# Gates spread by transfers, columns made by transposes, row fills issued later, and a reordered last slot in a two-layer encoder kernel

## The reference

```python
mod = c_act @ ada_w[layer] + ada_b[layer]
sh_m, sc_m, g_m, sh_f, sc_f, g_f = split(mod, 6)
h = rms_norm(x, norm_mix_g[layer]) * (1 + sc_m) + sh_m
x = x + g_m * token_mixer(h, ...)      # 2304-column projection, window + differential attention, w_out
h = rms_norm(x, norm_ffn_g[layer]) * (1 + sc_f) + sh_f
y = swiglu(h, ...) if layer == 0 else moe_swiglu(h, ...)   # dense 3584 wide; or top 2 of 8 experts
x = x + g_f * y
# at the end: rms_norm(x, final_g)
```

## Time and profile before

| | |
|---|---|
| median of three runs | 1755.93 us |
| the profiled execution, its own time | 1757.38 us |
| its span, first to last instruction | 1755.6 us |
| mean granted TensorE clock | 0.963 |
| PE / DVE / ACT / POOL busy | 1639.4 / 1302.5 / 1024.1 / 29.7 us (93 / 74 / 58 / 2%) |
| DMA | 544.83 MB, 310 GB/s over the span |

### The profile page before, as it was taken

One profiled execution on the slowest core, in us unless ns is written; L12 is line 12 of the kernel. 1 busy time (PEld: TensorE's weight loads), 2 busy tenths in 40 slices (PEclk: granted clock), 3 DMA queues, 4 the chain that ended last, 5 costly groups with the idle time before them and its releaser, 6 DMA issues.

```text
span 1755.6 us, 20351 instructions
## 1 busy us (share of the span) xinstructions
PE 1639.4 (93%) x7699; PEld 1314.7 (75%) x7700; DVE 1302.5 (74%) x997; ACT 1024.1 (58%) x760; POOL 29.7 (2%) x35
## 2 busy tenths in 40 slices
PE   3988889999798778999999999999999999999996
PEld 1755678878684667888888888888888888888884
DVE  2856644355475568898888888988898888888885
ACT  2324443354334435777777777767777767677772
POOL 0000000000000001000000000000000000000002
PEclk7899799999899689999999999999999999999998
DMA  9578576436168228999999999999999999999992
GB/s 366 199 290 331 214 291 227 152 143 223 64 216 334 98 97 349 368 381 389 372 391 378 370 386 373 387 388 374 387 378 376 394 362 387 385 376 390 380 373 73
DMA packets 161471, 544.83 MB, mean 310 GB/s; under 512 B 9704, under 2 KB 12432, under 8 KB 155280
## 3 DMA queue, kind: packets, MB, share of 16 engines
q1 hardware_dynamic: 154416, 528.01, 78.7%
q10 hardware_dynamic: 5856, 11.99, 1.9%
q0 software_dynamic: 1152, 4.19, 0.7%
HBM read 528.43 MB, written 15.73 MB: 310 GB/s over the span
## 4 chain that ended last, share of the span: by engine, by line
PE 84%; DVE 7%; ACT 3%; DMA 2%; issue 2%; POOL 1%; ACTq 1%; DVEq 0%; POOLq 0%
PE ps L1562 25%; PE ps L1564 25%; PE ps L1563 25%; DVE weights_lo L953 2%; PE ps L1521 2%; PE ps L1809 2%; DMA lamv<-in_lam_k_dram 1%; PE ps L1641 1%; DVE tmp L1051 1%; DMA weights<-in_ada_w_dram 1%; PE ps L1629 1%; PE ps L1533 1%; PE ps L1552 0%; PE ps L1617 0%; PE ps L1780 0%
## 5 line engine op out<-in xcount | busy, mean ns | idle before, releaser
L1249 DVE TENSOR_TENSOR raw_lo<-raw,raw_hi 128x4096 fp32r<-128x4096 f32 x188 | 831.2, 4425 | 143.2 <-ACT raw_hi L783 140.7
L783 ACT ACTIVATE raw_hi<-raw 128x4096 fp32r<-128x4096 f32 x188 | 683.3, 3635 | 221.4 <-PE ps L1564 221.4
L1562 PE MATMUL ps<-raw_hi,hT_hi 128*128 128x512 f32 x1008 | 397.5, 394 | 0.8 <-DVE hT_lo L1439 0.8
L1564 PE MATMUL ps<-raw_hi,hT_lo 128*128 128x512 f32 x1008 | 393.6, 390 | 0.0
L1563 PE MATMUL ps<-raw_lo,hT_hi 128*128 128x512 f32 x1008 | 393.1, 390 | 0.0
L1564 PEld LDWEIGHTS ps<-raw_hi,hT_lo 128*128 128x128 f32 x1008 | 189.7, 188 | 40.0
L1562 PEld LDWEIGHTS ps<-raw_hi,hT_hi 128*128 128x128 f32 x1008 | 189.9, 188 | 38.9 <-DVE hT_lo L1439 1.0
L1563 PEld LDWEIGHTS ps<-raw_lo,hT_hi 128*128 128x128 f32 x1008 | 190.0, 189 | 38.1
L1562 PE MATMUL ps<-raw_hi,m_actT_hi 128*128 128x512 f32 x504 | 196.2, 389 | 1.2 <-DVE m_actT_lo L1255 1.2
L1564 PE MATMUL ps<-raw_hi,m_actT_lo 128*128 128x512 f32 x504 | 196.3, 390 | 0.0
L1563 PE MATMUL ps<-raw_lo,m_actT_hi 128*128 128x512 f32 x504 | 196.1, 389 | 0.0
(11 more groups left out here) (223 smaller groups left out, 1352.5 us busy)
## 6 DMA issues: line engine op xcount, KB each, us to landing
raw<-in_moe_w_gate_dram SPq DMA_DIRECT2D x126, 1024.0 KB, 6.0
raw<-in_moe_w_up_dram SPq DMA_DIRECT2D x126, 1024.0 KB, 8.3
raw<-in_moe_w_down_dram SPq DMA_DIRECT2D x126, 1024.0 KB, 7.0
weights<-in_ada_w_dram SPq DMA_DIRECT2D x24, 2048.0 KB, 10.7
weights<-in_w_in_dram SPq DMA_DIRECT2D x8, 2048.0 KB, 9.9
weights<-in_ffn_w_gate_dram SPq DMA_DIRECT2D x14, 1024.0 KB, 6.4
weights<-in_ffn_w_up_dram SPq DMA_DIRECT2D x14, 1024.0 KB, 8.6
weights<-in_ffn_w_down_dram SPq DMA_DIRECT2D x7, 2048.0 KB, 10.3
```

Source lines behind the costliest of these rows:

```text
L783: act.activation(raw_hi[HIGH_OF[p]][:], raw[RAW_OF[p]][:], ACT.Copy).then_inc(m_hi, 1)
L1249: dve.tensor_tensor(raw_lo[r][:], raw[r][:], raw_hi[h][:].bitcast(F32), ALU.subtract).then_inc(m_lo, 1)
L1562: pe.matmul(dst, stat_hi, hi, start=start, stop=False, skip_group_check=True)
L1564: return pe.matmul(dst, stat_lo, hi, start=False, stop=stop, skip_group_check=True)
```

## The change

It has six parts. Gates: POOL issues eight transfers for each gate (`spread_gate`), each from one group of 32 partitions of modrow to 32 partitions of `gate`; the matmuls, the four ACT copies and PE's wait are gone, and DVE waits for the transfers (`gate_mix`, `gate_ff`). Columns: PE transposes whole pieces of modrow into a PSUM bank of its own for each round, and DVE copies one of 32 columns. ACT: `straight("out", layer, 1)` stands right after `split_transposed`. Fills: ACT issues the two fills after its part of the first dense block, not before it. Slots: SP issues the gate and up loads of phase 1 ahead of the load of the rows. End: `gated_output` comes ahead of `earlier_slots`.

```diff
+        COLUMN_ROUNDS = [((0, 0, 0),), ((0, 1, 0), (0, 2, 1), (1, 0, 6)), ((1, 1, 0), (1, 2, 1))]
...
@@ sync: slot
                 for n in range(NPH):
+                    for p in GU_AT[n]:
+                        room(p)
+                        load_gate_up(e, n, p)
                     if n == 1:
                         sp.wait_ge(rows_put, 16 * 2 * NT)
...
-                    for p in GU_AT[n]:
-                        room(p)
-                        load_gate_up(e, n, p)
@@ gpsimd
+            def spread_gate(layer, which):
+                r, done = 1 + which, (gate_mix, gate_ff)[which]
+                pool.wait_ge(mod_ready, 3 * layer + r + 1)
+                for h in range(2):
+                    g = 2 * which + h
+                    for j in range(4):
+                        pool.dma_start(gate[32 * j:32 * j + 32, which, 512 * h:512 * h + 512],
+                                       modrow[32 * g:32 * g + 32, r, :]).then_inc(done, 16)
             for layer in range(DEPTH):
                 norm(2 * layer)
                 for t in range(NT):
+                    spread_gate(layer, t)
                     pool.wait_ge(dms_done, NT * layer + t + 1)
@@ scalar
-            def gates(layer):
-                for i in range(4):
-                    act.wait_ge(gates_ps, 4 * layer + i + 1)
-                    act.activation(gate[:, i // 2, (i % 2) * 512:(i % 2) * 512 + 512], ps[:, 4 + i, :],
-                                   ACT.Copy).then_inc(gates_ready, 1)
...
                 one(0, False)
+                act.dma_start(x_rows.rearrange("s p n -> p s n"),
+                              fing[:].unsqueeze(1).broadcast_to([P, N_SLOT + 1, D])).then_inc(rows_filled, 16)
+                act.dma_start(y_rows[N_EXP - 1:].rearrange("s p n -> p s n"),
+                              fing[:].unsqueeze(1).broadcast_to([P, MAX_OVER + 1, D])).then_inc(rows_filled, 16)
...
                 split_transposed(3 * layer + 1)
-                gates(layer)
+                straight("out", layer, 1)
...
                     act.wait_ge(cols_ps, 2)
+                    act.wait_ge(gate_mix, 8 * 16)
+                    act.wait_ge(gate_ff, 8 * 16)
...
-                straight("out", layer, 1)
...
                 if not layer:
-                    act.dma_start(x_rows ...)
-                    act.dma_start(y_rows ...)
                     dense()
@@ vector
-                for layer, (a, b) in NEW_KINDS[n]:
-                    i = dve.tensor_copy(modc[:, layer, a:b], ps[:, 0, KD * a:KD * b].rearrange(
-                        "p (a k) -> p a k", a=b - a))
+                for layer, r, bank in COLUMN_ROUNDS[n]:
+                    i = dve.tensor_copy(modc[:, layer, 2 * r:2 * r + 2, :].rearrange("p a (b i) -> p (a b) i", i=4),
+                                        ps[:, bank, :].rearrange("p (i g x) -> p g i x", g=4, x=32)[:, :, :, 0])
...
                 act_turned(slots * NPH, WIDE[3])
+                gated_output(slots + (-1), slots * CHUNKS)
                 earlier_slots()
-                gated_output(slots + (-1), slots * CHUNKS)
...
-                dve.wait_ge(gates_ready, 4 * layer + 4)
+                dve.wait_ge(gate_mix, 8 * 16 * (layer + 1))
                 mixed(layer)
@@ tensor
+                for _, r, bank in COLUMN_ROUNDS[n]:
                     for i in range(4):
-                        mm = pe.matmul(ps[:, 0, 16 * r + i:16 * r + i + 13:4], modrow[:, r, i * P:i * P + P],
-                                       ident[:, 0:P:32], start=True, stop=True)
+                        mm = pe.transpose(ps[:, bank, i * P:i * P + P], modrow[:, r, i * P:i * P + P], ident[:])
...
                 mod_columns(layer + 1)
-                gates(layer)
-                pe.wait_ge(gates_ready, 4 * layer + 4)
                 for c in range(OUT_CHUNKS):
+                    if c:
+                        pe.wait_ge(cols_ready, layer + 2)
                     project("out", layer, c, 3 * layer + 1)
```

More of the change, by code:

```diff
@@ L332, in build @@
         ada_used, mod_ready, cols_ps, cols_ready = sem("ada_used"), sem("mod_ready"), sem("cols_ps"), sem("cols_ready")
-        gates_ps, gates_ready = sem("gates_ps"), sem("gates_ready")
+        gate_mix, gate_ff = sem("gate_mix"), sem("gate_ff")
         sq_done, ms_done, rstd_done, xn_done = sem("sq_done"), sem("ms_done"), sem("rstd_done"), sem("xn_done")
@@ L916, in _ @@
                 if not layer:
-                    act.dma_start(x_rows.rearrange("s p n -> p s n"),
-                                  fing[:].unsqueeze(1).broadcast_to([P, N_SLOT + 1, D])).then_inc(rows_filled, 16)
-                    act.dma_start(y_rows[N_EXP - 1:].rearrange("s p n -> p s n"),
-                                  fing[:].unsqueeze(1).broadcast_to([P, MAX_OVER + 1, D])).then_inc(rows_filled, 16)
                     dense()
@@ L1334, in dense_out @@
             def dense_out():
+                dve.wait_ge(gate_ff, 8 * 16)
                 for t in range(NT):
@@ L1488, in _ @@
             dve.memset(done_mark[:], 0.0).then_inc(y_stored, 16)
+            dve.wait_ge(gate_ff, 8 * 16 * DEPTH)
             first_input(0)
@@ L1526, in mod_columns @@
             def mod_columns(n):
-                rounds = ((0,), (1, 2, 0), (1, 2))[n]
                 pe.wait_ge(mod_ready, (1, 4, 6)[n])
-                for r in rounds:
+                for _, r, bank in COLUMN_ROUNDS[n]:
                     for i in range(4):
-                        mm = pe.matmul(ps[:, 0, 16 * r + i:16 * r + i + 13:4], modrow[:, r, i * P:i * P + P],
-                                       ident[:, 0:P:32], start=True, stop=True)
+                        mm = pe.transpose(ps[:, bank, i * P:i * P + P], modrow[:, r, i * P:i * P + P], ident[:])
                 mm.then_inc(cols_ps, 1)
-            def gates(layer):
-                for i, chunk in enumerate((4, 5, 10, 11)):
-                    g, r = chunk % 4, chunk // 4
-                    pe.matmul(ps[:, 4 + i, :], ones[32 * g:32 * g + 1, :], modrow[32 * g:32 * g + 1, r, :],
-                              start=True, stop=True).then_inc(gates_ps, 1)
             def transpose_all(n):
```

## The result

The changed kernel takes 1729.08 us, the median of four runs (1727.17 to 1731.18), against 1755.51 for the kernel before on the same chip: ratio 0.9852, 95% interval 0.9838 to 0.9866.

The account below looks back on a forecast made before the run. PE was taken to bound the kernel (busy 93% of the span, 84% of the wait chain). Terms -6.1 - 5.6 - 0.9 - 3.2 - 1.6 + 2.0 - 4.3 = -19.7 took 1757.38 to 1737.7, less 1.45: 1736 us, range 1730 to 1743.

Parts of the forecast that it names:

- Columns and gates: Between PE's last x transpose and the output projection: the gap shrinks to the new transposes, gaining 6.1 and 5.6 us.
- The clock at the output projections: Start of the output projection in both layers: the sum left the clock as it was, counting no gain.
- the rival that named this effect: Output projections: the clock rises by the first matmul, saving 5.3 us over both layers, for 1730.7 us; chance 0.10.
- First columns: First modulation columns: four transposes take 0.98 us where four matmuls took 1.87, gaining 0.9 us.
- Fills leave block 0: First dense block: PE's wait falls from 4.24 to 1.0 us, gaining 3.2, and the clock dip goes, gaining 1.6.
- Fills come to block 2: Dense block 2: the fills share the rate with weight loads and the second load comes late, costing 2.0 us.
- Gate transfers: POOL in attention: sixteen issues a layer at 0.98 + 0.30 to 1.95 us each do not delay rstd_d; cost nothing.
- slot loads: Expert slots: weights loaded ahead of the rows give nothing, since the load was already there in time.
- POOL's case: Rival in attention: issues take longer than 2.1 us, rstd_d is late; at 4.3 us 69 lost, 1805; chance 0.06.
- The end: Last slot: ysb is made before the gathered rows are summed, so the final additions end earlier, gaining 4.3 us.

Follow-up runs that it names:

- Columns by matmul: The changed kernel, but the modulation columns come from matmuls on 4 columns of the identity again, gates still spread by transfers; 1738.07 us, ratio 0.9907.
- the added transposes: The kernel of Columns by matmul with 16 unneeded 128-column transposes between columns and output projection in each layer; 1740.53 us, ratio 0.9922.

## Why the prediction was right or wrong

- **Columns and gates, -6.1 and -5.6: 7.6 and 6.7.** The first step that failed, in its price. The gap closed as said, and the wait for the copies was covered. But a transpose was priced at the half clock of the earlier trace rows, 0.246, and took 1.94/12 = 0.16 and, in layer 1, 1.08/8 = 0.14; the gaps of the earlier trace rows shrank to 1.69 and 0.84, where 2.95 and 1.97 were allowed.
- **The clock at the output projections, in the sum at nothing: 2.5 and 1.8.** The larger failure, and the step that the forecast broke on. The sum left the projections at the clock that they had, and the rival that named this effect (1730.7, worked out at 5.3 us, 4.3 measured) got 0.10. It was put aside because "PE was busy with small matmuls for 6.93, and the clock stayed at 0.50 through all of it", but those were matmuls on 4 columns and on one row, which the change takes out. The row spoke for work that is no longer there. Columns by matmul and, in layer 0, the added transposes show it: the same place at 0.50 with the one, at 1.00 behind the other. In all nine traces with full-width columns and nothing behind them the clock was up for the first matmul of both projections; the 4-column matmuls left it at 0.50 in five places of six, and the sixth is layer 1 of the run with added transposes. The Trainium skill, "TensorE: Matmul & The Clock Gate", "Part 4: PE-mode transpose", says that transposes don't count as activity in this way; here the traces disagree: the clock was 0.50 ahead of the sixteen added ones in layer 0 and 1.00 behind them. Without this rule the rival would have deserved an even chance, and the range would have reached lower. That the rival's 1730.7 lies so near the median is partly luck: it has 25.0 us for the pair of traces, which are 30.2 apart, and the medians are 3.8 closer than the traces.
- **First columns, -0.9: 0.8.** Right.
- **Fills leave block 0, -3.2 and -1.6: 4.9 together.** Right, with the clock at 1.00 behind it (214 to 218). The wait shrank to 0.30 and not to 1.0, so this run does not show what a wait of 1.0 does to the clock.
- **Fills come to block 2, +2.0: +0.5.** The second mis-sized term. The load was late by 0.85 us, not 1.7, no dip of the clock followed, and PE had part of it in hand. The share was as forecast, a third; the rate was not. From 245 to 265 us:

```profile
DMA packets 2747, 8.32 MB, mean 416 GB/s; under 512 B 48, under 2 KB 48, under 8 KB 2746
...
q10 hardware_dynamic: 1372, 5.55, 67.6%
q1 hardware_dynamic: 1374, 2.75, 35.4%
```

  The engines moved 416 GB/s where I had taken 369, the mean of a stretch with emptier ends. At a third of 416, two loads of 4.2 MB take 30 us, not 33. And the equal counts, 1372 and 1374, mend what I said of the Trainium skill, "DMA: Bandwidth & Descriptors", "Queues, rings and completion order": counted in the profile's packets, the queues do take equal turns. The fills' packets are 5.55 MB/1372 = 4 KB, the weights' 2 KB, hence a third of the bytes. The trace agrees with equal turns; whether these packets are what the page calls one, no run shows. My reading "the trace disagrees" took bytes for turns.
- **Gate transfers, 0; slot loads, 0.** Right for the time: 0.53 us an issue, below the 0.98 that I took; slots with the caveat above. Two slips: the put of 5.11 us ended 0.8 us behind the TENSOR_TENSOR, not with it (1727.69 against 1726.87), and POOL's case at 4.3 us comes to 68 us and 1804, not 69 and 1805.
- **The end, -4.3: 5.0 in the traces; the run that undoes it gives 4.0 by medians and 3.7 in its trace.** Right.
- **Not forecast:** layer 0's input projection took 1.6 us less; all later traces have 54.4 us there, and only that of before 56.1. It has half-clock matmuls from 53 to 56, behind a pause of 1.85 us, where the changed kernel has none behind one of 2.69; whether the 0.8 us of earlier start did that or chance is open. In slot 0 the half-clock stretch is shorter. Against them stand the +1.7 of layer 1's attention.

The four mis-sized terms are 1.5 + 1.1 + 4.3 + 1.5 = 8.4 of the 10.5 us between the sum (19.7) and the two traces (30.2); the medians are 6.9 us from the forecast (1736 - 1729.1).

## What to carry to other kernels

A half clock read in a stretch belongs to the work that filled the stretch: where a change replaces that work, price what follows at both clocks and give the faster one a real chance. Take narrow matmuls and pauses together out of the way to a large product: here the first alone kept the slow clock in both layers, and a pause alone brought it back in one of two. When two DMA queues meet, count packets and their sizes, and use the rate of a full stretch, not the mean over a landing time.

## What the runs showed of the hardware that was not expected

- TensorE's clock came up to 2.4 GHz over full-width fp32 transposes, even of a constant (layer 0: 0.54 while they ran, 1.00 behind them). It did not over 24 records of 4-column matmuls without a gap (0.50), yet where it had just come up, 16 records of them ran at 1.00.
- POOL issued 21 plain transfers at 0.5 us each and then stood, in four groups of four, for 1.92 to 11.14 us; eight at a time never stood.
- Indirect puts on POOL took 5.12 and 4.64 us beside DVE's 4.42 us TENSOR_TENSOR, and 0.98 to 1.12 without it.
- Layer 1's attention took 61.2 to 65.4 us in eleven traces of kernels with the same instructions in it. In the two traces of the changed kernel a half-clock stretch in it goes with 1.7 of the 2.8 us by which they differ.
